# ScalarE's copy of the turned weights, ahead of the exponentials of the newest pair

## The reference, cut to what matters

```python
# layer "ab": 8 heads over 256 keys, causal, beside a gated MLP
s = jnp.where(mask, s.astype(jnp.float32) * scale, NEG)
p = jax.nn.softmax(s, axis=-1).astype(v.dtype)
outs.append(jnp.einsum('bhqk,bkhd->bqhd', p, v[:, :q1]))
# layer "nsa": 16 heads, three branches (compressed, selected, window), gated sum
o = gates[:, :, 0] * o_cmp + gates[:, :, 1] * o_slc + gates[:, :, 2] * o_win
# layer "gqa": 16 heads, 4 key heads, 256 own + 256 context keys, no mask
s = jnp.einsum('bqkgd,bskd->bkgqs', q, k).astype(jnp.float32) * ATTN_SCALE
p = jax.nn.softmax(s, axis=-1).astype(v.dtype)
return jnp.einsum('bkgqs,bskd->bqkgd', p, v)
```

## Time and profile before

| | |
|---|---|
| median of three runs | 1870.11 us |
| profiled execution, its own time | 1869.12 us |
| its span | 1867.4 us |
| PE busy | 1508.5 us, 81% |
| DVE busy | 459.3 us, 25% |
| ACT busy | 243.7 us, 13% |
| chain that ended last | PE 45%, DMA 45%, DVE 5%, issue 2%, ACT 2% |
| DMA | 711.03 MB, mean 381 GB/s |
| attention loops in the span | ab 69.6 to 90.8, nsa 406.8 to 486.7, gqa 803.5 to 878.6 us |

### The profile page before, as it was taken

One profiled execution on the slowest core, in us unless ns is written; L12 is line 12 of the kernel. 1 busy time (PEld: TensorE's weight loads), 2 busy tenths in 40 slices (PEclk: granted clock), 3 DMA queues, 4 the chain that ended last, 5 costly groups with the idle time before them and its releaser, 6 DMA issues.

```text
span 1867.4 us, 22822 instructions
## 1 busy us (share of the span) xinstructions
PE 1508.5 (81%) x9954; PEld 716.4 (38%) x9954; DVE 459.3 (25%) x980; ACT 243.7 (13%) x524; POOL 83.6 (4%) x136
## 2 busy tenths in 40 slices
PE   8998777999999778989978677786799667667685
PEld 5654434764454434445522213221264222122221
DVE  2441011467421113874400000000043000000001
ACT  0410000126222011154100000000011000000000
POOL 1100000202000000111100000000000000000000
PEclk9999899999999899999998878887899878778787
DMA  7589999999579999597799999999988999999997
GB/s 294 211 308 426 426 427 424 373 355 372 211 287 419 426 426 421 181 410 288 270 429 431 431 430 430 431 431 430 420 349 335 430 430 431 430 431 430 432 426 291
DMA packets 114541, 711.03 MB, mean 381 GB/s; under 512 B 8240, under 2 KB 13344, under 8 KB 73472
## 3 DMA queue, kind: packets, MB, share of 16 engines
q1 hardware_dynamic: 108208, 697.14, 90.3%
q0 software_dynamic: 4128, 9.73, 1.5%
q10 hardware_dynamic: 2096, 2.57, 0.4%
HBM read 708.17 MB, written 1.05 MB: 380 GB/s over the span
## 4 chain that ended last, share of the span: by engine, by line
PE 45%; DMA 45%; DVE 5%; issue 2%; ACT 2%; SPq 1%; POOL 0%; DVEq 0%; ACTq 0%; PEldq 0%; POOLq 0%
DMA ring<-in_moe_w 23%; DMA work<-in_moe_w 9%; PE pb L809 8%; DMA ring<-in_moe_w_down 7%; PE pa L841 6%; DMA work<-in_moe_w_down 3%; PE acc L1512 3%; PE pb L788 2%; PE acc L1506 2%; PE acc L927 2%; PE pa L863 2%; PE acc L1410 2%; PE acc L1399 1%; PE acc L1227 1%; DMA mod<-in_moe_w_up 1%
## 5 line engine op out<-in xcount | busy, mean ns | idle before, releaser
L809 PE MATMUL pb<-ring,XT 128*32 128x256 f32 (+1 forms) x2528 | 340.1, 520 | 85.7 <-DMA ring<-in_moe_w 78.6
L841 PE MATMUL pa<-ring,work 128*32 128x512 f32 x928 | 197.2, 713 | 62.6 <-DMA ring<-in_moe_w 40.0
L809 PEld LDWEIGHTS pb<-ring,XT 128*32 128x32 f32 x2528 | 104.5, 116 | 286.9 <-issue 135.9
L809 PE MATMUL pb<-work,XT 128*32 128x512 f32 (+1 forms) x544 | 140.5, 613 | 20.9 <-DMA work<-in_moe_w 20.5
L974 DVE TENSOR_TENSOR work<-work,pb 128x256 f32<-128x256 f32 (+1 forms) x32 | 17.8, 555 | 548.9 <-PE pb L809 442.6
L927 PE MATMUL acc<-XT,work 128*128 128x512 f32 x256 | 118.4, 605 | 32.3 <-DVE XT L990 19.4
L863 PE MATMUL pa<-work,HM 128*128 128x128 f32 x896 | 113.0, 288 | 16.3 <-issue 16.3
L863 PEld LDWEIGHTS pa<-work,HM 128*128 128x128 f32 x896 | 112.1, 204 | 31.1 <-issue 31.1
L841 PE MATMUL pa<-work 128*32 128x512 f32 x320 | 94.7, 735 | 25.5 <-DMA work<-in_moe_w 16.7
L936 ACT COPY XT<-pa 128x512 f32<-128x512 f32 x32 | 18.8, 586 | 703.0 <-PE pa L863 694.4
L841 PEld LDWEIGHTS pa<-ring,work 128*32 128x32 f32 x928 | 43.1, 127 | 167.5 <-issue 75.1
(11 more groups left out here) (426 smaller groups left out, 1759.8 us busy)
## 6 DMA issues: line engine op xcount, KB each, us to landing
ring<-in_moe_w SPq DMA_DIRECT2D x135, 2048.0 KB
work<-in_moe_w SPq DMA_DIRECT2D x46, 2048.0 KB
ring<-in_moe_w_up SPq DMA_DIRECT2D x28, 2048.0 KB
ring<-in_moe_w_gate SPq DMA_DIRECT2D x26, 2048.0 KB
ring<-in_moe_w_down SPq DMA_DIRECT2D x24, 2048.0 KB
ring<-in_w_mod SPq DMA_DIRECT2D x40, 1024.0 KB
mod<-in_moe_w SPq DMA_DIRECT2D x11, 2048.0 KB
work<-in_moe_w_down SPq DMA_DIRECT2D x8, 2048.0 KB
```

Of the source, the lines that this page charges most:

```text
L809: last = nc.tensor.matmul(hbank[m][j * CAP:(j + 1) * CAP, :], m_xg[:, k, j * CAP:(j + 1) * CAP], slot_of(per * m + j // held)[:, at:at + f ...
L841: last = nc.tensor.matmul(pa[j * CAP:(j + 1) * CAP, h, :], m_ht[:, c, j * CAP:(j + 1) * CAP], slot_of(i)[:, at:at + 512], start=(c == 0), ...
```

## The change

In `att_scalar` the copy of the transposed weights of pair i-2, with its waits, moves ahead of the exponentials of pair i. The wait on `s_pt` that stood before the exponentials goes, since the copy has waited for the same count. No instruction is added or removed on any engine, and the copy has the same source, target and size.

```diff
             for i in range(n + 3):
+                j = i - 2
+                if 0 <= j < n:
+                    act.wait_ge(s_pt, n0 + j + 1)
+                    if j >= 2:
+                        act.wait_ge(s_pv, n0 + j - 1)
+                    w = sp["width"](j)
+                    nc.scalar.copy(sp["pt"][:, j % 2, 0:w], acc[:, 1, 0:w]).then_inc(s_ptc, 1)
                 if i < n:
                     act.wait_ge(s_max, n0 + i + 1)
-                    if i >= 2:
-                        act.wait_ge(s_pt, n0 + i - 1)
...
                     last.then_inc(s_exp, 1)
-                j = i - 2
-                if 0 <= j < n:
-                    act.wait_ge(s_pt, n0 + j + 1)
-                    if j >= 2:
-                        act.wait_ge(s_pv, n0 + j - 1)
-                    w = sp["width"](j)
-                    nc.scalar.copy(sp["pt"][:, j % 2, 0:w], acc[:, 1, 0:w]).then_inc(s_ptc, 1)
```

## The result

| kernel | median us | lowest to highest | runs | ratio to before |
|---|---|---|---|---|
| before | 1869.48 | 1866.94 to 1871.41 | 6 | |
| changed | 1858.95 | 1858.11 to 1861.87 | 6 | 0.9948 (0.9935 to 0.9961) |

The kernel became faster, by 10.5 us between these medians, and by 7 to 12 us within the interval of the ratio. The forecast was 1862. The two profiled executions lie closer together: 1869.12 before and 1861.87 after, 7.25 apart; the one after happens to be the slowest of its six. The changed kernel was timed again beside the kernel before, twice: 1857.02 (5 runs, ratio 0.9941, 0.9926 to 0.9955; 11 us) and 1861.58 (8 runs, 0.9961, 0.9948 to 0.9974; 7.3 us).

The account below looks back on a forecast made before the run. TensorE's transposes waited 7.7 us for the copy, and what follows hangs on each loop's end. Gains of 0.15 (ab) + 4.1 (nsa) + 3.7 (gqa) = 8.0 us give 1862.1 on the median, forecast 1862, range 1858.5 to 1866.5.

Parts of the forecast that it names:

- gqa without a block: gqa steps without a modulation block: pitch falls from 3.66 to TensorE's own 3.10, four waits go, 2.4 us gained.
- The slacks: gqa steps without a block: transposes have 0.4 us to spare after exponentials and maxima, the copy of results 0.1 every second step.
- rival 1: Only plain waits go; VectorE or the copy of results binds in gqa and nsa; 5.4 us gained, 1864.7; chance 0.11.
- gqa, start: Step 3 of gqa: transposes waited 1.06 for the copy, 1.1 us goes; steps 6 and 7 another 0.2.
- Steps with a block: Steps with a modulation block: gqa pitch stays 4.96; four even nsa steps gain 0.2 each, 0.8 us.
- nsa without a block: Last nsa steps: VectorE late next at 3.27 a step, 2.0 us gained; then TensorE binds alone, 1.5 us more.
- ab: The ab loop: one wait of 0.16 goes, 0.15 us gained, bounds 0 to 0.2.
- One us saved in a loop is one us of the total: After each attention loop: the projection and resumed loads hang on its end, so they move with it; 8.0 us in all.
- Signs: Expected in later profiles: loops ab 21.0, nsa 75.8, gqa 71.4 us; SyncE's waits at loop ends stay 26 to 30.
- Rivals 2 and 3: Weights set the loops' ends, about 1869, chance 0.08; late exponentials lengthen 14 steps with a block, 1876, chance 0.03.
- 4: Copy beside the values' matmuls becomes 0.2 longer than 1.01, time still 1862; chance counted within the main case's 0.78.

Follow-up runs that it names:

- the kernel with nsa's blocks earlier: Changed kernel with each modulation block of nsa one step earlier (steps 0 to 8 instead of 1 to 9); 1858.68 us, ratio 0.9929.
- the sixteen copies: Changed kernel with 16 more ScalarE copies of the last pair's result at the end of the gqa loop; 1868.3 us, ratio 0.9988.
- the repeated exponentials: Changed kernel with ScalarE doing part of the exponentials twice in most steps with a block, same result; 1860.52 us, ratio 0.9931.
- the kernel with ScalarE's first copy moved: Changed kernel with nsa's modulation blocks one step earlier and ScalarE's copy for the first block before the first exponentials; 1859.84 us, ratio 0.9949.
- nsa alone: Kernel before with the copy ahead of the exponentials only in the nsa loop; 1865.39 us, ratio 0.9979.

## Why the prediction was right

The time fell where the prediction put it, and by the mechanism that it named. How near the number came is in part luck: the median of 1858.95 lies 0.5 above the lower end of the range, the second comparison's 1857.02 lies below it, and the third's 1861.58 almost on the forecast. The mechanism rests on the steps below and not on the total. By its steps:

- *gqa without a block*: right. Pitch 3.11 for 3.10, and 2.39 us for 2.4. The slacks held: the one of 0.4 measured 0.43, and the one of 0.1 was 0.38, because ScalarE's work of a step ends 4.81 after the scores and not 5.05. No transposes wait for the scaling in gqa after the first, so rival 1 did not come.
- *gqa, start*: right; the wait of 1.1 stays when only the later steps are changed, and goes in the changed kernel. The 0.2 estimated for steps 6 and 7 was 0.17 (a pitch of 3.87 became 3.70). The sum was 3.7, measured 3.65.
- *Steps with a block*: right, 4.96 before and after, and in nsa's even ones 1.06 became 0.86. Four of these give 0.8; measured to the scores of step 11, 0.79.
- *nsa without a block*: VectorE was named rightly as what is late next, its size was not; and it is late for two pairs of transposes, while TensorE sets the time of the third. VectorE's turn was costed at 3.27, the recorded busy stretch of 3.16 and a hop of 0.11; from mask to mask it takes 457.56 - 454.48 = 3.08. A turn begins before the recorded end of the one before, so adding a hop went the wrong way. The third pair's transposes (those at 464.92 in the earlier trace rows) were to come 2.6 us sooner, 3 x 0.2 and 2.0; they come 58.06 us after the loop's first scores before and 54.99 after, 3.07 sooner. The term of 2.0 was thus 2.5. From there to the last but one transposes it is 13.06 before and 11.47 after, 1.59 for the predicted 1.5. nsa in all 4.6 for 4.1.
- *ab*: 0.47 for 0.15, outside its own bounds of 0 to 0.2. Its second and third transposes are 3.37 apart (80.15 to 83.52 us), and were 3.72 (81.06 to 84.78). The one recorded wait of 0.16 stood for 0.35, and the rest lies in steps without a recorded wait. The same hidden part that the prediction had added in nsa and gqa was left out here.
- *One us saved in a loop is one us of the total*: not contradicted, and borne out for a delay at the end of gqa. The sum was 8.0, the loops gave 8.7 (8.6 by the second profile of before), and the three comparisons 7.3 to 11.0 by their ratios, each with an uncertainty of some 2.5. Whether anything beyond the 8.7 is real stays open: the rest of the kernel varies by 5 us between profiles.
- *Signs*: the loops were to be 21.0, 75.8 and 71.4 and were 20.65, 75.15 and 72.39. gqa's is 1 longer than forecast for the first scores at half the clock and not for a step of the sum: in the kernel with nsa's blocks earlier, whose gqa code is the same and which started at the full clock, the loop is 71.44. SyncE's waits were to stay at 26 to 30; that of gqa fell to 25.2.

The Trainium skill, "Perfetto Trace Analysis", section "Optimization Strategy", had by the recorded gaps alone led to 7.7 us. The gaps did close once the copy that ended them came sooner; the 8.7 measured differ from that sum by the unrecorded parts of waits, less the 0.6 that VectorE keeps in nsa (0.23 and 0.33 above).

The rivals: 1 is refuted by the pitch in gqa. Its price was also too high: two turns of VectorE, each 0.33 longer, are 0.7 us and not the 1.2 that it took, so its time should have been some 1864.2. Rivals 2 and 3 had the time at 1869 and 1876, which the measured time alone excludes; the sixteen copies and the repeated exponentials show why, within what they test. Of 4, the copy's median duration is 1.012 for 1.009 before, so there is no slower copy.

## What to carry to other kernels

When an engine runs in order and serves two buffers, put first the operation that another engine is about to need, and second the one whose user waits for a third engine anyway; the work that it does is the same, and here that alone took 0.5% off. Cost such a move by writing down one step's chain twice, with and without the moved piece, and take what is late next (here TensorE itself in gqa and VectorE in nsa) as the new pitch, instead of adding up the recorded waits: those miss some 0.05 to 0.2 a step. To see whether a saving of 8 us is there, compare stretches between two instructions of the loop, which repeated to 0.2 and better here, and not totals, in which work that wasn't touched varied by 5.

## What the runs showed of the hardware

TensorE's granted clock at the start of a loop is not always the same. In gqa the first scores took 2.08 in the changed kernel and 1.13 in the kernel before, after the same pause of 2.80 and 8 matmuls of line 1217:

```profile
797.48 2.08 PE L1391 MATMUL pa<-work 64*128 64x512 f32 x4
```

```profile
803.54 1.13 PE L1391 MATMUL pa<-work 64*128 64x512 f32 x4
```

The windows on those stretches give the clock (length, busy of PE, PEld, DVE, ACT, POOL, granted clock, DMA share, GB/s): 0.50, which is 1.2 GHz, in the changed kernel, and 1.00, 2.4 GHz, before.

```profile
797.00:800.00 3.00, 3.00 (x10) 1.19 (x8) 0.39 (x1) 1.87 (x2) 2.62 (x3) 0.50 1.05 408
```

```profile
803.00:806.00 3.00, 3.00 (x24) 0.93 (x20) 1.28 (x2) 1.89 (x3) 3.00 (x3) 1.00 1.05 410
```

In nsa the first large block of 16 matmuls took 3.64 in the changed kernel and 1.92 in the kernel with ScalarE's first copy moved, where TensorE had worked without a pause since 409.31:

```profile
413.99 3.64 PE L1227 MATMUL acc<-ring,work 128*32 128x512 f32 x16
```

```profile
413.53 1.92 PE L1227 MATMUL acc<-ring,work 128*32 128x512 f32 x16
```

The kernel before shows both levels for that block in its two profiles, 3.64 and then 1.92, and its loop was 79.84 and then 78.65. In the first, TensorE had waited 2.09 us for ScalarE and the clock was low for the work that followed; in the second the first scores were already at the low clock (1.65 for 0.93) and full clock was back after a pause of 1.37. So in nsa one and the same kernel shows both. In gqa, both profiles of before have the first scores at 1.13, and the three of the changed kernel have them at 2.08, 2.08 and 1.66. The order in the gqa loop alone doesn't decide it, as the kernel with nsa alone (gqa in the old order) and the one with nsa's blocks earlier (gqa in the new order) show:

```profile
798.37 2.08 PE L1391 MATMUL pa<-work 64*128 64x512 f32 x4
```

```profile
795.48 1.13 PE L1391 MATMUL pa<-work 64*128 64x512 f32 x4
```

Whether the change makes the low start of gqa more frequent stays open. A difference of a microsecond between two loops can come from the clock alone, so whole loops are best compared at the same level. With nsa's first large block at 3.64 the loop is 79.84 before and 75.15 to 75.30 changed; with it at 1.92, 78.65 before and 74.05 with nsa alone. With gqa's first scores at 1.13 it is 75.08 before and 71.44 in the new order; with them at 2.08, 76.02 in the old order and 72.39 in the new. At either level that is 4.5 to 4.7 us for nsa and 3.6 for gqa, the gain of the stretches.

An operation of VectorE can start sooner than the recorded end of the one ahead: in nsa the scaling that starts at 456.61 is recorded until 457.64, and the next mask starts at 457.56. So a turn of VectorE is 3.08 where the recorded stretch of one is 3.16 long.
